# A fourth weight block held on chip through half of each mixture-of-experts stage, in the buffers of the transposed rows and of h

## The reference, cut to what matters

```
for i in range(2):
    h = h + mixer_i(rms_norm(h, g_mix[i]))             # convolution module, then attention
    h = h + hier_moe(rms_norm(h, g_ffn[i]), ...)       # top-1 of 4 groups, then top-2 of its 8 experts
    gate = sigmoid(rms_norm(h, g_ple[i]) @ ple_w_gate[i])
    h = h + gate * (p[i] @ ple_w_proj[i])

def expert_block(xblk, e):                             # w_gate, w_up: 1024 x 512, w_down: 512 x 1024
    return (silu(xblk @ w_gate[e]) * (xblk @ w_up[e])) @ w_down[e]
```

## Time and profile before

| | |
|---|---|
| median of 3 runs | 1335.97 us (1334.55 to 1336.41) |
| the profiled execution | 1336.18 us, of which 1334.1 us are the span of the profile |
| PE busy | 1035.9 us, 78% of the span |
| DVE, ACT, POOL busy | 24%, 23%, 34% |
| DMA | 449.24 MB, a mean of 337 GB/s over the span |
| mean granted clock of PE | 0.896 of full speed |

### The profile page before, as it was taken

How to read it: one execution, slowest core, us unless ns; L and a number is a source line. 1 busy time by engine, 2 the same in 40 slices (tenths; PEclk the granted TensorE clock), 3 DMA queues, 4 the chain that set the end, 5 groups by cost and what they waited for, 6 DMA issues and landing times.

```text
span 1334.1 us, 27871 instructions
## 1 busy us (share of the span) xinstructions
PE 1035.9 (78%) x10412; PEld 591.8 (44%) x10413; DVE 316.9 (24%) x886; ACT 302.5 (23%) x710; POOL 453.5 (34%) x743
## 2 busy tenths in 40 slices
PE   6968877667777776778998889787777777777678
PEld 5744544333444333334454555443333444334443
DVE  3994300000120000005136771210000121001111
ACT  5873311111111111112113561211111111112121
POOL 2340164443455334330000130454344354343520
PEclk9989988888889888888999699898888889889989
DMA  9952399999999999998415503699999999999980
GB/s 304 380 193 65 117 400 428 429 428 429 428 429 428 429 427 430 427 419 318 132 63 188 254 25 153 253 400 426 431 426 430 426 430 427 430 427 421 429 357 31
DMA packets 62872, 449.24 MB, mean 337 GB/s; under 512 B 10841, under 2 KB 21713, under 8 KB 38256
## 3 DMA queue, kind: packets, MB, share of 16 engines
q1 hardware_dynamic: 57776, 448.25, 81.2%
q10 hardware_dynamic: 5056, 0.48, 0.3%
HBM read 447.66 MB, written 1.05 MB: 336 GB/s over the span
## 4 chain that ended last, share of the span: by engine, by line
DMA 44%; PE 39%; DVE 9%; issue 4%; ACT 3%; SPq 1%; POOL 0%; ACTq 0%; DVEq 0%
DMA ring<-in_moe_w_up 43%; PE PS L560 15%; PE PS L445 10%; PE PS L539 2%; PE PS L575 2%; ACT arena L1131 1%; PE PS L547 1%; PE PS L582 1%; DVE hn L1399 1%; PE PS L433 1%; PE PS L729 1%; DVE arena L1399 1%; DVE ppw L1742 1%; SPq L318 1%; PE PS L600 1%
## 5 line engine op out<-in xcount | busy, mean ns | idle before, releaser
L560 PE MATMUL PS<-ring,arena 128*32 128x256 f32 x4160 | 334.5, 486 | 190.5 <-DMA ring<-in_moe_w_up 166.2
L560 PEld LDWEIGHTS PS<-ring,arena 128*32 128x32 f32 x4160 | 161.5, 134 | 355.3 <-issue 218.2
L1451 DVE TENSOR_TENSOR arena<-PS,arena 64x256 f32<-64x256 f32 x65 | 27.8, 428 | 590.9 <-ACT arena L1195 585.1
L575 PE MATMUL PS<-ring,arena 128*32 128x256 f32 x2080 | 125.7, 381 | 30.8 <-DVE arena L1454 30.8
L1195 ACT ACTIVATE arena<-PS 64x256 f32<-64x256 f32 x64 | 24.2, 377 | 515.6 <-PE PS L560 515.6
L966 POOL TENSOR_SCALAR arena<-arena 128x32 f32<-128x32 f32 x64 | 18.9, 295 | 291.3 <-PE PS L547 285.8
L925 POOL TENSOR_SCALAR arena<-arena 128x512 f32<-128x512 f32 x67 | 105.7, 1578 | 24.8 <-POOL arena L972 12.9
L575 PEld LDWEIGHTS PS<-ring,arena 128*32 128x32 f32 x2080 | 73.1, 109 | 61.1 <-issue 37.4
L919 POOL TENSOR_SCALAR arena<-arena 128x32 f32<-128x32 f32 x260 | 88.7, 364 | 13.1 <-POOL arena L966 12.9
L927 POOL TENSOR_TENSOR arena<-arena 128x512 f32<-128x512 f32 x67 | 85.6, 1278 | 5.6
L582 PE MATMUL PS<-arena 32*128 32x256 f32 x1040 | 74.5, 397 | 6.6 <-ACT arena L1193 0.6
(11 more groups left out here) (323 smaller groups left out, 1209.5 us busy)
## 6 DMA issues: line engine op xcount, KB each, us to landing
ring<-in_moe_w_gate SPq DMA_DIRECT2D x62, 2048.0 KB, 17.9
ring<-in_moe_w_up SPq DMA_DIRECT2D x62, 2048.0 KB, 22.3
ring<-in_moe_w_down SPq DMA_DIRECT2D x62, 2048.0 KB, 24.0
wb<-in_ple_w_gate SPq DMA_DIRECT2D x4, 2048.0 KB, 32.5
ring<-in_conv_w_pw SPq DMA_DIRECT2D x3, 2048.0 KB, 19.0
ring<-in_nsa_w_in SPq DMA_DIRECT2D x3, 2048.0 KB, 15.0
wb<-in_moe_w_gate SPq DMA_DIRECT2D x2, 2048.0 KB, 14.7
wb<-in_moe_w_up SPq DMA_DIRECT2D x2, 2048.0 KB, 13.2
```

Source lines behind the costliest of these rows:

```text
L560: i = pe.matmul(PS[32 * j:32 * j + 32, BGU, 0:256].rearrange("q (p c) -> q p c", c=2), xT[:, k, :], w[:, k, :].rearrange("q (p h c) -> q h ...
L575: i = pe.matmul(PS[32 * j:32 * j + 32, BY, 0:Q4], hT[:, c, 32 * f:32 * f + 32], w_dn(s)[:, f, c, Q4 * j:Q4 * (j + 1)], start=(q == 0), sto ...
L1451: return v.tensor_tensor(hh[64:128, :], PS[64:128, BGU, 0:256], gs[64:128, :], ALU.mult)
```

## The change

A fourth third, gate of e19, is held. It is loaded as two halves of 1 MiB: into the buffer `xnT` once the router's product has read it (`rt_mm`), and into the buffer `h` once ACT has copied `h` to PSUM (`acc_ok`). Both loads stand on SP's queue ahead of those of e2. The regular load of gate of e19 is left out. DVE copies the two halves into slot 1 of the ring behind its steps for e17. DVE's wait for the held thirds, behind its steps for e14, now counts five transfers and not three. In layer 1 the load of up of e1 moves forward, from behind `out_mm` 8 to directly behind the embedding inputs.

```diff
+HN_AT = [1, 2, 3, 4, 5, 6]
...
+        HX = [xnT[:, :, :].rearrange("p k q -> p (k q)"), h[:, :, :].rearrange("p t d -> p (t d)")]
...
                 m = HELD // 2
+                spare = moe_w_gate[L, HELD + 3].rearrange("(p k) f -> p (k f)", k=8)
+                sp.wait_ge(rt_mm, L + 1)
+                sp.dma_start(HX[0], spare[:, 0:2048]).then_inc(held_in, 16)
+                sp.wait_ge(hn_dve, HN_AT[3 * L + 1])
+                sp.wait_ge(acc_ok, 4 * (L + 1))
+                sp.dma_start(HX[1], spare[:, 2048:4096]).then_inc(held_in, 16)
                 with sp.Fori(1, m) as it:
                     pair(it)
                 pair(m, (0, 1))
-                pair(m + 1, (2, None))
+                pair(m + 1, (2, 0))
...
             embeddings(1)
+            gate_up_load(1, 1, R1[1], 1, gu_in[1])
             sp.wait_ge(out_mm, 7)
             gate_up_load(1, HELD, WB[0], 0, held_in)
             sp.wait_ge(out_mm, 8)
             gate_up_load(1, 1, R1[0], 0, gu_in[1])
-            gate_up_load(1, 1, R1[1], 1, gu_in[1])
             gate_up_load(1, HELD + 1, WB[1], 1, held_in)
             experts(1)
...
                 expert_steps(m - 1, 0)
-                dve.wait_ge(held_in, 48 * (L + 1))
+                dve.wait_ge(held_in, 80 * (L + 1))
                 dve.wait_ge(gu_mm, NE * L + HELD - 1)
                 v.tensor_copy(R0[0], WB[0]).then_inc(gu_in[0], 16)
...
                 expert_steps(m, 1)
+                for i_ in range(2):
+                    i = v.tensor_copy(R1[0][:, 2048 * i_:2048 * (i_ + 1)], HX[i_])
+                i.then_inc(gu_in[1], 16)
                 with dve.Fori(m + 1, NE // 2) as it:
```

## The result

The changed kernel takes 1326.34 us in the median of 4 runs (1324.29 to 1329.65), the kernel before 1335.26 in the median of its 4 by then: a ratio of 0.9944, with a 95% interval of 0.9922 to 0.9966. It was measured twice more, beside other variants: 1323.71 against 1334.04 (0.9921, 0.9894 to 0.9948) and 1323.43 against 1333.77 (0.9914, 0.9901 to 0.9927). By the medians it is 8.9, 10.3 and 10.3 us faster, by the interval of the first ratio 4.5 to 10.4.

A forecast was written before the change was run, and what follows sets the result against it. DMA was taken to bound the long expert stretches. Terms -4.9 in layer 0 and -4.9 + 0.1 in layer 1 sum to -9.7, from a 1336.18 profiled run to 1326.5, or 1326.3 in the median; range 1323.7 to 1329.4.

The forecast's parts named there:

- The price of a third: Expert stretches: one 2 MiB load fewer on the saturated queue saves 4.89 us in each layer, -9.8 in all.
- Rival E: Expert stretches: a third costs 5.86 us, so two give 11.7 and the time is 1324.3; chance 0.02.
- The load put in and the move: Start of the expert stages: two halves, 2.4 us each, and the moved up load fit DMA's idle time, cost 0.
- Rivals C and D: Start of expert stages: C, halves not free or another bound, 1336, chance 0.04; D, late `acc_ok`, 1341.6, chance 0.03.
- e2's loads behind 164.5: Start of layer 0's experts: these loads issued after 164.5 would show the prediction wrong.
- The walk through e18 to e21: Layer 0's held stretch: the last three products start at about 415.7, 425.9 and 439.7, the last gaining the full 4.9 us.
- rival B: Held stretch: PE paces it and issues depend on its progress, losing one layer's gain, 1331.1; chance 0.07.
- a DMA dip: Held stretch, after the left out load: a dip in DMA's rate would show the prediction wrong.
- the 0.6 allowed: The gate issue of e20 in the held stretch: a dry queue loses 0 to 0.6 us in layer 1; 0.1 taken.
- The copies, 2.4 us, and their cover: DVE in the held stretch: two copies take 2.4 us, at most 4.6, hidden; PE has 3.6 us in hand.
- POOL: Beside DVE's copies in layer 0: POOL's chain is pushed back 1.2 us, at most 3.4, cost 0.
- the clock's way into the time: Last expert's product of each layer: PE's clock shifts it, -3.6 to +1.9 us in all at the outside.

The follow-up runs named there:

- e19: Not a run: the expert whose gate load the change leaves out of the queue and holds instead; forecast to start at about 415.7 in layer 0.
- layer0_only: The changed kernel with the half loads, the left out load and the copies in layer 0 only: 1329.74 us, 0.9963 of the kernel before.
- left_out_only: The changed kernel without half loads and copies, the regular gate load still left out (output wrong): 1324.84 us, 0.9940 of the kernel before.
- held_e21: The changed kernel with the gate third of an expert two places later held as the fourth: 1327.78 us, 0.9946 of the kernel before.
- left_out_3: Gate loads of three consecutive experts left out, nothing in their place (output wrong): 1309.26 us, 0.9801 of the kernel before.
- e28: Not a run: an expert around whose loads in layer 1 the queue runs dry for a moment; its gate load was issued with a lead of 3.4 us.
- extra_halves: The changed kernel with the regular gate load kept, the halves loaded but never copied or used: 1333.66 us, 0.9995 of the kernel before.
- move_only: The kernel before with only layer 1's early up load moved forward: 1334.66 us, 1.0000 of the kernel before.
- halves_late: The changed kernel with the two halves issued later, where the queue is saturated: 1332.55 us, 0.9991 of the kernel before.
- e20: Not a run: the expert after e19; its product in layer 0 started on a DMA wait at 429.96 before the change.
- after_again: A repeat of the changed kernel, nothing altered: 1323.71 us, 0.9921 of the kernel before.
- after_third: A third measurement and profile of the changed kernel, nothing altered: 1323.43 us, 0.9914 of the kernel before.
- copies_x3: The changed kernel with each of DVE's two copies of the halves made three times: 1323.85 us, 0.9928 of the kernel before.
- e22: Not a run: an expert behind the held stretch, where PE in layer 0 of copies_x3 waits for DMA for 4 us again.
- e31: Not a run: the last expert of each layer; its product in layer 0 took 5.62 us in the kernel before.
- spread_4_5: The changed kernel with the fourth third and a further half third (in `ppw`) held for later, spread out experts, second PE loop: 1327.80 us, 0.9957 of before.
- held_4_5: The changed kernel with half a gate third more held in `ppw` and a second PE loop: 1326.67 us, 0.9944 of the kernel before.

## Why the prediction was right

*The price of a third, 4.89 us: right.* layer0_only, left_out_only and held_e21 give 4.84 to 4.88 in layer 0, left_out_3 4.82 and 4.90 for each of three. In layer 1 left_out_only and held_e21 give 5.11 and 5.22 by D, of which 0.3 is what before lost at e28; without that part it is 4.8 and 5.0. Rival E, a third at 5.86 us, is out.
The Trainium skill, "DMA: Bandwidth & Descriptors", section "Specifications", has the limit of about 358 GB/s behind that rival. The trace disagrees with it: the long stretches of experts ran at 427 to 429 GB/s in both kernels above.

*The load put in and the move, cost 0: right.* extra_halves 0.9995, move_only 1.0000, and halves_late shows that the cover is what the gain consists of. Rivals C and D did not come about: e2's loads went out 9.3 us behind the second half in both layers. The sign that I had named, e2's loads behind 164.5, did show (165.02), and means nothing: they waited for e0's product, not for the halves.

*The walk through e18 to e21: right in its end, off in between (layer 0).* I had e19 at 415.7, e20 at 425.9, e21 at 439.7. They came at 418.69, 429.47 and 440.37. The product of e18 took 6.61 us, at the slow clock (0.54 granted from 408 to 412), where it had taken 3.89, so PE was 3 us later than worked out, and gate of e20 was issued at 412.54, 3.0 us ahead of the end of the transfers in front (405.73 + 9.79 = 415.52). DMA dipped, as in the earlier trace rows:

```profile
412.00:416.00 4.00, 3.44 (x58) 1.90 (x50) 0.72 (x2) 0.75 (x2) 1.98 (x6) 1.00 0.84 295
```

That is rival B's mechanism, and a DMA dip was a sign of being wrong on my list, but its price was small. It came in layer 0 and not in layer 1 where I looked for it, and only in this profile: B is 377.22, 0.4 more than held_e21's 376.80, while after_again, whose product of e18 took 5.26 us, and after_third have 376.78 and 376.89. My formula for such a dip, 4 x (1 - 295/429) = 1.2 us, is three times what the stretch lost. In layer 1 I took 0.1. There the lead was 3.6 us (issued at 1099.34, transfers in front done at 1093.15 + 9.79 = 1102.9), and e18 to e21 gave 34.29 for seven thirds, 4.90 each: nothing lost. The 0.4 is within the 0.6 allowed.

*The copies, 2.4 us, and their cover: right.* 1.22 us each, and copies_x3 shows that 4.5 us of delay at e19 cost nothing. I had written that PE has 3.6 us in hand at e21 and that what exceeds it is lost. The first is borne out (e21 came 1.3 us behind its data, 442.79 against 407.22 + 7 x 4.89 = 441.5), the second is wrong: what is left over at e21 is made up at e22, since the queue stays filled.

*POOL: right.* 1.1 us later, and nobody waited.

*The sum.* Worked out -9.7; the stretches of the three profiles give -4.5, -4.9, -4.8 for B and -4.4, -4.8, -4.7 for D, so -8.9 to -9.7. The three medians are 8.9, 10.3 and 10.3 below before. That the median came out at 1326.34 for a forecast of 1326.3 is luck: single runs spread over more than 11 us, before itself had sunk from 1335.97 to 1335.26 by then, and the two later medians are 1323.71 and 1323.43. The second of these lies under the stated range. The range was added up wrongly: 1326.3 - 2.6 - 1 gives 1322.7 at the lower end and not 1323.7.

The rest goes with the clock, and for C it can be followed a part of the way. The same program ran in 1317.55 us at a mean granted clock of 0.906 and in 1328.53 at 0.897. C is 3.9 us longer in the profile of 1329.65 than in that of after_again. Where it lies can be read from e31 of layer 0, e0 and e5 of layer 1; first after (its e31 and e5 are above), then after_again:

```profile
846.59 2.70 PE L569 MATMUL PS<-ring,arena 128*32 128x256 f32 x41 [0.69 <-DVE arena L1455]
```

```profile
584.58 5.18 PE L569 MATMUL PS<-ring,arena 128*32 128x256 f32 x64 [3.44 <-DMA ring<-in_moe_w_up]
...
839.92 2.67 PE L569 MATMUL PS<-ring,arena 128*32 128x256 f32 x41 [1.30 <-DVE arena L1455]
...
905.37 5.19 PE L569 MATMUL PS<-ring,arena 128*32 128x256 f32 x64 [3.59 <-DMA ring<-in_moe_w_up]
```

From e31 to e0 it is 259.40 against 255.34 us, from e0 to e5 65.31 against 65.45. So the whole difference lies ahead of layer 1's experts: 1.2 us in the product of e31 itself (6.35 against 5.18), and most of the rest in the attention, where the granted clock from 725 to 737 was 0.67 and in the same steps of after_again (720 to 732) 0.81. Among the experts the clock differed too (0.74 against 1.00 from 862 to 882), and it cost nothing, since e5 waits for DMA. Over the fourteen profiles the time from e31 to the start of ACT's copy of h in layer 1 runs from 246.6 to 252.8 us, with the changed kernel alone at 249.3 to 252.8. What sets it in a given run is not shown. I had named only the last products of the layers as the clock's way into the time, with -3.6 to +1.9 us at the outside. That term was too small: the attention ahead of the experts brings in more.

## What to carry to other kernels

Where a transfer queue is the bound, what counts is the bytes that stand on it since it was last idle: find the idle stretches, move bytes there, and price each by the time between two landings. A delay on another engine costs nothing as long as the next issue comes well before the queue is empty (here a lead of 3.0 us was too short by 0.4 us, one of 3.6 us was enough), so look for the lead of each issue and not for the engine's own wait. To judge a gain of a few us, measure between two events that start on the same kind of wait; the whole time carries the noise of every other stage.

## What was not expected of the hardware

DVE's copies and POOL's steps slow each other, not only POOL: beside POOL's work a 128x2048 copy took 1.51 to 2.19 us and not 1.22, and POOL's 128x512 step 3.06 and not 1.58 (rows of copies_x3 above).
The Trainium skill, "SBUF — State Buffer", section "SBUF: two separate sides", has a lock that is held for one whole instruction by whichever engine starts first, and the other blocks; the trace agrees in that both sides take longer. It does not show strict turns: from 406.43 to 414.45 in copies_x3 the three POOL steps and the rest of the copies would need 9.4 us one after the other at their undisturbed lengths (1.58, 1.30 and 0.74; 1.22 per copy), and 8.0 passed.

PE can sit for 4 to 7 us ahead of a loop's first product with no releaser shown (6.96 us in spread_4_5, 4.28 in held_4_5; in after_third it is 0.56 and ends on DVE). In every kernel here it sits 2.6 to 5.9 us ahead of the first e1 of layer 0. The cause is argued here, not shown.
